# The matmuls of 256 columns take their columns in the order of lines 0, 8, 1, 9 up to 7, 15

## The chip, the cores and the metric

One of the eight cores of a Trainium2 chip runs the whole kernel. The metric is the time of one execution in microseconds (us) of device time, as the median of the runs. TensorE multiplies a stationary tile of weights, loaded beforehand, by a moving tile that streams past, and adds into PSUM; VectorE (DVE), ScalarE (ACT) and GpSimd (POOL) do the elementwise work, and SyncE (SP) issues the loads.

## The reference

Two layers on 256 tokens of width 2048, in float32. All large products have this form, with the weights read once from the chip's main memory:

```python
# layer 1: latent attention beside a gated convolution
h = rmsnorm(x, pre_norm_g)
q_a, c_kv, k_rope, z_mla, c_in, b_gate, c_gate, z_conv, g_mla, g_conv = split(h @ w_in)
q, kv = rmsnorm(q_a) @ w_q_b, rmsnorm(c_kv) @ w_kv_b
attn = causal_attention(q, kv, k_rope) * silu(z_mla)
y_conv = (b_gate * conv3(c_gate * c_in) * silu(z_conv)) @ w_o_conv
merged = sigmoid(g_mla) * (attn @ w_o_mla) + sigmoid(g_conv) * y_conv
x = x + rmsnorm(merged @ w_out, post_norm_g)
# layer 2: 16 meta tokens in front; top-k attention beside a chunked recurrence
h2 = rmsnorm(concat(meta, x))
parts = split(h2 @ w_in_2)
merged = sum over 2 branches of sigmoid(gate) * (y_branch @ w_branch_2)
out = x + merged @ w_out_2
```

## The kernel before

**The numbers.** Every float32 operand of a large product is split into a high and a low part in the format `float32r`, which TensorE takes in one pass, and a product is three matmuls: weights high by x high, weights high by x low, weights low by x high. They add up in one PSUM bank.

**The work in tiles.** The kernel keeps activations transposed: a tile has 128 features on the partitions and the tokens as columns. The tokens are 256 in layer 1 and in most of layer 2 (`S`), and 272 where the meta tokens take part (`T`). `phases` lists the products in order. A phase has groups of up to 512 weight columns, a group has its reduction in tiles of 128 rows, and a unit is what fits 1024 weight columns per partition: mostly two reduction tiles of 512 weight columns. A unit is loaded by SP into one of four slots of `w_raw` (`load`, 512 KB), ACT writes its high part into one of three slots of `w_hi` (`split_hi`, L1616), DVE the low part into `w_lo` (`split_lo`, L1919), and TensorE then runs `tile` (L1290) four times on it, once for each 128 weight columns: 2 reduction tiles of 3 matmuls in each, 24 for the unit. A slot comes free when TensorE is through with its unit.

**Who is stationary.** In the tiles of kind `f` a 128x128 block of weights is stationary and x moves, with 256 or 272 columns. In those of kind `t` (the last product, `wout2`, and half of `kv`) x is stationary and the weights move, with 512 or 256 columns. While a matmul streams, the weights of the next one are loaded beside it. All of them go through the helper `mm`, so the profile has them on L1281.

**Where the operands lie.** A line, here, is 64 bytes of a partition: 16 float32 columns. The allocations are made so:

```python
self.whi = sb("w_hi", [P, N_SPLIT, UNIT], F32R)
self.wlo = sb("w_lo", [P, N_SPLIT, UNIT], F32R)
hb = sb("hb", [P, ODD + 2 * KT * S + ODD], F32R)[:, ODD:ODD + 2 * KT * S]...
self.ob_hi, self.ob_lo = (sb(n, [P, KT, T + ODD], F32R)[:, :, 0:T] for n in ("ob_hi", "ob_lo"))
```

`ODD` is 16 columns, one line. A slot of `w_hi` is 64 lines, a block of weights in it 8 lines. `hb` holds the high and the low part of layer 1's operand, 16 lines a tile, and starts one line into its allocation. A tile of `ob_hi` or `ob_lo` takes 288 columns, 18 lines, of which `operand` (L1136) gives the 256 from column 16 on, or all 272. The results go to a PSUM bank at its start, or, in the phase with eight tiles, to its first or second half (`out_of`, L1149).

**What sets the order.** The whole program is a list of steps that `plan_work` writes once; each engine walks through it and takes the steps of its kind, with semaphores between the engines. Elementwise jobs and the small matmuls of attention and recurrence (plain float32, some of them read in pieces of 1 to 64 columns by `rec_level`) are put between the tiles.

Of the kernel before, what the change touches and what calls it, by code (L numbers as in the profile page):

```python
# [19 lines left out]
S = 256  # L20
# [188 lines left out]
COLS = lambda m: slice(m * P, (m + 1) * P)  # L209
# [831 lines left out]
N_LVL = len(LEVELS) * P // 2  # L1041
L0 = CONSTS["late"][0]

pair = lambda x: x.rearrange("p (h x) -> p h x", h=2)
four = lambda x: x.rearrange("p (a b) -> p a b", a=4)

# [226 lines left out]
def tensor_engine(nc, m, plan, S_):  # L1273
# [6 lines left out]
    def mm(dst, lhsT, rhs, start=True, stop=True):  # L1280
        return nc.tensor.matmul(dst, lhsT, rhs, start=start, stop=stop, skip_group_check=True)  # L1281

    def operand_ready(name, k):
        if name in ("h2", "h2_all"):
            pe.wait_ge(*done["meta"])
            pe.wait_ge(*done["h2", k])
        elif name in ("lat_q", "lat_kv", "oc", "zm", "mg", "ya", "yb", "mg2", "h"):
            pe.wait_ge(*done[name, k])

    def tile(s):  # L1290
        i, t = s.args
        u, slot = plan.units[i], i % N_SPLIT
        hi_w = m.whi[:, slot, 0:u.size].rearrange("p (k n) -> p k n", k=u.nk)
        lo_w = m.wlo[:, slot, 0:u.size].rearrange("p (k n) -> p k n", k=u.nk)
        if t == 0:
            pe.wait_ge(*plan.split[i]["w_lo"])
        if u.k0 == 0:
            pe.wait_ge(*s.of["bank"].after)
        dst = m.out_of(u, t, s.of["bank"].slot)
        kind, j = u.tiles[t][0], int(u.tiles[t][1])  # L1300
        for k in range(u.nk):
            kt = u.k0 + k
            operand_ready(u.phase.operand, kt)
            x_hi, x_lo = m.operand(u.phase.operand, kt)
            first, last = kt == 0 and not (len(u.tiles) > 4 and t % 2), kt == u.phase.ktiles - 1
            if kind == "f":
                inst = mm(dst, hi_w[:, k, COLS(j)], x_hi, first, False)
                inst = mm(dst, hi_w[:, k, COLS(j)], x_lo, False, False)
                inst = mm(dst, lo_w[:, k, COLS(j)], x_hi, False, last)
            else:  # L1310
                w_hi, w_lo, to = hi_w[:, k, :], lo_w[:, k, :], dst
                if u.phase.name == "kv":
                    w_hi, w_lo, to = heads_kv(w_hi), heads_kv(w_lo), pair(dst)
                inst = mm(to, x_hi[:, COLS(j)], w_hi, first, False)
                inst = mm(to, x_lo[:, COLS(j)], w_hi, False, False)
                inst = mm(to, x_hi[:, COLS(j)], w_lo, False, last)
        if u.last:
            inst.then_inc(S_("proj"), 1)
        elif t == len(u.tiles) - 1:
            inst.then_inc(S_("used"), 1)  # L1320
# [261 lines left out]
    def x1_turn(s):  # L1582
# [5 lines left out]
        turn(b[:, P:S], m.xT2[:, k, P:S], ident).then_inc(S_("x1_t"), 1)  # L1588

    does = dict(tile=tile, constants=constants, warm=warm, pre_cols=pre_cols, x_tile=x_tile, row_sum=row_sum, row_spread=row_spread,  # L1590
                cols=cols, angle=angle, meta_turn=meta_turn, rope=rope, scores1=scores1, turn1=turn1, mix1=mix1,
                ki_turn=ki_turn, qa_sum=qa_sum, tok_turn=tok_turn, index=index, scores2=scores2, turn2=turn2,
# [1012 lines left out]
```

## Time and profile before

| | before |
|---|---|
| median of 3 runs | 1965.05 us (1962.56 to 1965.1) |
| the profiled execution's own time | 1960.36 us |
| its span, first to last instruction | 1959.1 us |
| granted TensorE clock over the span | 0.997 of full |
| TensorE matmul busy | 1940.1 us, 99% |
| DVE, ACT, POOL busy | 60%, 45%, 16% |
| loaded from main memory | 335.09 MB, 174 GB/s over the span |

The span is the time between the first and the last instruction on the core; the execution's own time has some 1.3 us more around it. The page gives a matmul's length from its first column to its last result. Matmuls overlap, so a group's mean length is longer than the distance between two starts; that distance is read from the timeline, or from a piece of the chain divided by its count.

### The profile page before, as it was taken

How to read it: one execution, taken by the hardware profiler on the slowest of the kernel's cores; microseconds unless marked ns; L12 is line 12 of the kernel's file. 1: busy time of each engine (PE TensorE's matmuls, PEld its weight loads, DVE VectorE, ACT ScalarE, POOL GpSimd, SP SyncE). 2: the span in 40 equal slices, each digit the busy share in tenths (PEclk: the TensorE clock that was granted, in tenths of full speed). 3: DMA queues.
4: the chain of work that ended last, by engine and by line, in shares of the span. 5: the costliest groups of instructions: out<-in, count | busy, mean ns of one | idle time of the engine just before them, and what ended most of it. 6: DMA issues, size and time to landing. Idle time of an engine off the chain costs nothing.

```text
span 1959.1 us, 37135 instructions
## 1 busy us (share of the span) xinstructions
PE 1940.1 (99%) x15806; PEld 1906.0 (97%) x15806; DVE 1176.2 (60%) x1708; ACT 878.8 (45%) x1264; POOL 319.5 (16%) x320
## 2 busy tenths in 40 slices
PE   8999999999999999999999999999999999999999
PEld 8999999999999999999999999999999999999987
DVE  7765666555554555654564665676467786555644
ACT  6444454544444334444445433455443333444443
POOL 3210010101010002300122253040011232110200
PEclk9999999999999999999999999999999999999999
DMA  7565555556666566666565564444564444566564
GB/s 261 154 194 172 170 151 148 170 178 187 190 183 186 191 184 183 183 194 187 190 227 194 171 205 129 142 140 120 161 179 145 139 141 137 176 195 191 184 229 159
DMA packets 175919, 343.79 MB, mean 175 GB/s; under 512 B 10494, under 2 KB 19578, under 8 KB 175226
## 3 DMA queue, kind: packets, MB, share of 16 engines
q1 hardware_dynamic: 174106, 337.16, 56.5%
q10 hardware_dynamic: 1648, 4.26, 0.6%
q8 instruction: 124, 2.03, 0.4%
q14 instruction: 41, 0.34, 0.1%
HBM read 335.09 MB, written 6.29 MB: 174 GB/s over the span
## 4 chain that ended last, share of the span: by engine, by line
PE 91%; DVE 3%; issue 1%; ACT 1%; POOL 0%; POOLq 0%; DVEq 0%; ACTq 0%
PE bank L1281 91%; DVE w_lo L1919 1%; ACT w_hi L1616 0%; DVE arena L2194 0%; DVE hb L2155 0%; DVE scratch L2025 0%; DVE ob_lo L2199 0%; DVE arena L2188 0%; DVE ob_lo L2130 0%; DVE ob_lo L2155 0%; POOL scratch L2515 0%; PE bank L1498 0%; PE bank L1588 0%; PE bank L1437 0%; PE bank L1438 0%
## 5 line engine op out<-in xcount | busy, mean ns | idle before, releaser
L1919 DVE TENSOR_TENSOR w_lo<-w_raw,w_hi 128x1024 fp32r<-128x1024 f32 (+2 forms) x644 | 786.9, 1226 | 495.3 <-ACT w_hi L1616 493.7
L1616 ACT ACTIVATE w_hi<-w_raw 128x1024 fp32r<-128x1024 f32 (+2 forms) x644 | 662.5, 1032 | 894.7 <-PE bank L1281 888.7
L1281 PE MATMUL bank<-hb,w_hi 128*128 128x256 f32 x4896 | 870.1, 281 | 3.4 <-DVE w_lo L1919 3.3
L1281 PEld LDWEIGHTS bank<-hb,w_hi 128*128 128x128 f32 x4896 | 748.7, 188 | 6.3 <-DVE w_lo L1919 5.0
L1281 PE MATMUL bank<-hb,w_lo 128*128 128x256 f32 x2448 | 684.2, 280 | 0.0
L1281 PE MATMUL bank<-ob_hi,w_hi 128*128 128x256 f32 (+1 forms) x2224 | 643.0, 289 | 4.4 <-DVE w_lo L1919 3.9
L1281 PE MATMUL bank<-ob_lo,w_hi 128*128 128x256 f32 (+1 forms) x2224 | 627.0, 282 | 0.0
L1281 PE MATMUL bank<-ob_hi,w_lo 128*128 128x256 f32 (+1 forms) x2224 | 626.2, 282 | 0.0
L1281 PEld LDWEIGHTS bank<-hb,w_lo 128*128 128x128 f32 x2448 | 460.8, 188 | 0.0
L1281 PEld LDWEIGHTS bank<-ob_hi,w_hi 128*128 128x128 f32 x2224 | 419.6, 189 | 8.1 <-DVE w_lo L1919 5.4
L1281 PEld LDWEIGHTS bank<-ob_lo,w_hi 128*128 128x128 f32 x2224 | 419.5, 189 | 1.5
L1281 PEld LDWEIGHTS bank<-ob_hi,w_lo 128*128 128x128 f32 x2224 | 419.0, 188 | 0.0
L1281 PE MATMUL bank<-arena 128*128 128x64 f32 (+4 forms) x618 | 101.7, 302 | 2.6 <-ACT arena L1836 1.6
L1281 PEld LDWEIGHTS bank<-arena 128*128 128x128 f32 x618 | 81.0, 191 | 4.8 <-ACT arena L1836 2.3
L2525 POOL TENSOR_TENSOR arena<-scratch,arena 128x256 f32<-128x256 f32 x32 | 38.4, 1229 | 269.7 <-DVE scratch L2025 269.7
L2025 DVE TENSOR_TENSOR scratch<-bank,factor 128x256 f32<-128x256 f32 (+1 forms) x132 | 52.8, 422 | 38.1 <-PE bank L1281 38.0
L1281 PE MATMUL bank<-w_hi,ob_hi 128*128 128x512 f32 (+1 forms) x192 | 69.0, 360 | 0.0
L1281 PE MATMUL bank<-w_lo,ob_hi 128*128 128x512 f32 (+1 forms) x192 | 68.5, 357 | 0.0
L1281 PE MATMUL bank<-w_hi,ob_lo 128*128 128x512 f32 (+1 forms) x192 | 68.2, 355 | 0.0
L2498 POOL TENSOR_TENSOR arena<-arena,factor 128x256 f32<-128x256 f32 x16 | 19.2, 1233 | 268.9 <-DVE arena L2025 268.9
L2515 POOL TENSOR_TENSOR scratch<-scratch,head_factor 128x256 f32<-128x256 f32 x16 | 12.6, 786 | 238.7 <-ACT head_factor L1729 238.7
L2025 DVE TENSOR_TENSOR arena<-bank,factor 128x256 f32<-128x256 f32 (+1 forms) x86 | 34.5, 420 | 23.6 <-PE bank L1281 23.6
(240 smaller groups left out, 1174.0 us busy)
## 6 DMA issues: line engine op xcount, KB each, us to landing
w_raw<-in_w_in SPq DMA_DIRECT2D x436, 512.0 KB, 3.7
w_raw<-in_w_out SPq DMA_DIRECT2D x64, 512.0 KB, 4.2
w_raw<-in_w_o_conv SPq DMA_DIRECT2D x32, 512.0 KB, 3.9
w_raw<-in_w_o_mla SPq DMA_DIRECT2D x32, 512.0 KB, 4.1
w_raw<-in_w_branch SPq DMA_DIRECT2D x32, 512.0 KB, 3.8
w_raw<-in_w_kv_b SPq DMA_DIRECT2D x16, 512.0 KB, 3.7
w_raw<-in_w_q_b SPq DMA_DIRECT2D x16, 384.0 KB, 3.3
arena<-x_kept SPq DMA_DIRECT2D x2, 2048.0 KB, 10.1
```

The source lines that it names most:

```text
L1281: return nc.tensor.matmul(dst, lhsT, rhs, start=start, stop=stop, skip_group_check=True)
L1616: act(dst, src, ACT.Copy).then_inc(S_("w_hi"), 1)
L1919: tt(low, src, high.bitcast(F32), ALU.subtract).then_inc(S_("w_lo"), 1)
L2025: tt(dst, m.proj[s.of["pb"]][:, 0:dst.shape[1]], factor, ALU.mult).then_inc(S_("evac"), 1)
L2498: tt(m.u_t[:, t, :], m.u_t[:, t, :], m.R, ALU.mult).then_inc(S_("conv_b"), 1)
L2515: tt(z, z, ring[s.of["head"].slot][:, 0:S], ALU.mult).then_inc(S_("silu"), 1)
L2525: tt(y, m.scratch[s.of["scratch"].slot][:, 0:S], y, ALU.add).then_inc(S_("merged"), 1)
```

## The change

The columns of a moving tile of 256 are viewed as two halves of eight lines, and the access pattern goes over line, half, column within the line: line 0, line 8, line 1, line 9, up to line 7, line 15. The PSUM tile is viewed in the same way, so each result lands at the address it had before. It holds for all tiles of kind `f` with 256 columns. Those with 272 columns keep their order (in `twos`, a tile whose second dimension isn't `S` is handed back as it is), and so do those of kind `t`. The program has the same instructions in the same order on every engine.

```diff
+twos = lambda x: x.rearrange("p (b a e) -> p a b e", b=2, e=16) if x.shape[1] == S else x
 pair = lambda x: x.rearrange("p (h x) -> p h x", h=2)
...
             if kind == "f":
-                inst = mm(dst, hi_w[:, k, COLS(j)], x_hi, first, False)
-                inst = mm(dst, hi_w[:, k, COLS(j)], x_lo, False, False)
-                inst = mm(dst, lo_w[:, k, COLS(j)], x_hi, False, last)
+                x_hi, x_lo, to = twos(x_hi), twos(x_lo), twos(dst)
+                inst = mm(to, hi_w[:, k, COLS(j)], x_hi, first, False)
+                inst = mm(to, hi_w[:, k, COLS(j)], x_lo, False, False)
+                inst = mm(to, lo_w[:, k, COLS(j)], x_hi, False, last)
```

## Rows read from the trace of the kernel before

**Rows 1.** The page: engines and their busy share, granted clock by slice, chain by engine.

```profile
PE 1940.1 (99%) x15806; PEld 1906.0 (97%) x15806; DVE 1176.2 (60%) x1708; ACT 878.8 (45%) x1264; POOL 319.5 (16%) x320
...
PEclk9999999999999999999999999999999999999999
...
PE 91%; DVE 3%; issue 1%; ACT 1%; POOL 0%; POOLq 0%; DVEq 0%; ACTq 0%
```

**Rows 2.** The chain in order of time: start us, length us, what; its four longest pieces.

```profile
79.53 108.86 PE bank L1281 x918
...
388.05 163.46 PE bank L1281 x1384
...
561.44 239.63 PE bank L1281 x2040
...
832.54 257.56 PE bank L1281 x2212
```

**Rows 3.** Waits of TensorE: us in total, times, longest us; the costliest.

```profile
PE bank L1281 <- DVE w_lo L1919: 7.1, 7, 2.8
```

**Rows 4.** Groups by shape: matmuls; count | busy us, mean ns of one | idle us before.

```profile
L1281 PE MATMUL bank<-hb,w_hi 128*128 128x256 f32 x4896 | 870.1, 281 | 3.4 <-DVE w_lo L1919 3.3
...
L1281 PE MATMUL bank<-hb,w_lo 128*128 128x256 f32 x2448 | 684.2, 280 | 0.0
...
L1281 PE MATMUL bank<-ob_hi,w_hi 128*128 128x256 f32 x1824 | 521.2, 286 | 4.4 <-DVE w_lo L1919 3.9 <-DVE ob_lo L2199 0.4
L1281 PE MATMUL bank<-ob_lo,w_hi 128*128 128x256 f32 x1824 | 511.8, 281 | 0.0
L1281 PE MATMUL bank<-ob_hi,w_lo 128*128 128x256 f32 x1824 | 510.6, 280 | 0.0
...
L1281 PE MATMUL bank<-ob_hi,w_hi 128*128 128x272 f32 x400 | 121.8, 305 | 0.0
```

**Rows 5.** Timeline, TensorE, near 1323 and 1472 us: start us, us for all xcount.

```profile
1323.35 0.49 PE L1498 MATMUL bank<-con,prob 128*128 128x128 f32 x3
...
1472.24 1.00 PE L1281 MATMUL bank<-arena 128*128 128x64 f32 x8
```

**Rows 6.** Groups by shape again: the f32 matmuls of 64 and 128 columns.

```profile
L1281 PE MATMUL bank<-arena 128*128 128x64 f32 x224 | 28.1, 268 | 1.1 <-POOL arena L2555 1.1
L1281 PE MATMUL bank<-arena 128*128 128x128 f32 x192 | 26.0, 275 | 0.0
...
L1498 PE MATMUL bank<-con,prob 128*128 128x128 f32 x24 | 3.9, 273 | 0.0
```

**Rows 7.** Timeline, TensorE, 1141 us, first and last of five starts.

```profile
1141.12 0.42 PE L1281 MATMUL bank<-ob_lo,w_hi 128*128 128x256 f32 x1
...
1141.97 0.42 PE L1281 MATMUL bank<-ob_hi,w_lo 128*128 128x256 f32 x1
```

**Rows 8.** Busy time in windows: us, busy of each engine (x), PEclk, DMA share, GB/s.

```profile
1141.50:1142.50 1.00, 1.00 (x7) 1.00 (x6) 0.32 (x1) 0.00 (x0) 0.90 (x1) 0.56 0.52 131
1144.50:1145.50 1.00, 1.00 (x11) 1.00 (x10) 1.00 (x1) 0.11 (x1) 0.00 (x0) 1.00 1.26 312
```

**Rows 9.** Timeline, TensorE, 1106 us, first and last of 18 starts.

```profile
1105.96 0.28 PE L1281 MATMUL bank<-ob_hi,w_hi 128*128 128x256 f32 x1
...
1107.89 0.28 PE L1281 MATMUL bank<-ob_hi,w_lo 128*128 128x256 f32 x1
```

**Rows 10.** Groups by shape: the two halves of a weight unit on DVE and ACT.

```profile
L1919 DVE TENSOR_TENSOR w_lo<-w_raw,w_hi 128x1024 fp32r<-128x1024 f32 x612 | 767.0, 1256 | 494.3 <-ACT w_hi L1616 492.7
...
L1616 ACT ACTIVATE w_hi<-w_raw 128x1024 fp32r<-128x1024 f32 x612 | 647.5, 1059 | 873.2 <-PE bank L1281 867.2 <-DMA w_raw<-in_w_out 5.5
```

**Rows 11.** Timeline, TensorE, last phase, first and last of 14 starts.

```profile
1919.95 0.39 PE L1281 MATMUL bank<-w_hi,ob_lo 128*128 128x512 f32 x1
...
1922.98 0.40 PE L1281 MATMUL bank<-w_lo,ob_hi 128*128 128x512 f32 x1
```

## The prediction

> **What bounds the kernel now.** I read the share of busy time first: TensorE is busy for 99% of the span and its granted clock stands at 2.4 GHz in nearly every slice [rows 1]. Busy time alone proves little, since matmuls overlap, so the chain of work that ended last comes next. It runs over TensorE for 91% of the span, through the one line that issues the matmuls [rows 1]. Of the waits of TensorE that the trace names, the largest sum is 7.1 us in 7 waits, for the low halves of the weights [rows 3]. So the time is the number of matmuls times the distance between two starts, and only that distance can change much.
>
> The matmuls that the change touches are those with a moving tile of 256 columns. The groups by shape give 4896 + 2448 on `hb` and 3 x 1824 on `ob_hi` and `ob_lo`, together **12,816** [rows 4]. The 280 ns that such a row shows is the length of one from first column to last result; what counts is the distance of starts. Four long pieces of the chain hold almost nothing else: 108.86 + 163.46 + 239.63 + 257.56 = 769.51 us for 918 + 1384 + 2040 + 2212 = 6554 matmuls, or **117.4 ns** each [rows 2].
>
> What could it be? Two rows give a floor. Three transposes in a row, each of which loads 128 columns of weights and streams 128 columns of f32, take 0.49 us; with the last one's own length of 273 ns taken off, 2 distances make 0.217 us, **109 ns** each [rows 5, 6]. Eight matmuls that stream only 64 columns behind a weight load of 128 take 1.00 us, or 105 ns each with the last one's 268 ns off, so it is the weight load that counts there [rows 5, 6]. Each matmul of 256 columns also has one weight load of 128 columns beside it, so 109 ns is what the weight side allows. The moving side: in the short stretch where the granted clock fell to 1.2 GHz (0.56 on the mean of that microsecond) [rows 8], four distances of the same 256-column shape make 0.85 us, 212.5 ns, which is 256 columns at 1.2 GHz and nothing more [rows 7]. At 2.4 GHz this is 106.3 ns. So at the slow clock there is no excess over the columns, and at the fast clock there is one of 8 ns over the floor of 109. Something that has slack at half pace has none at full pace.
>
> And the excess isn't fixed. In the stretch from 1105.96 to 1107.89 us, 17 distances of this shape, with the same kind of tiles and the same program line, make 1.93 us: 113.5 ns [rows 9]. The piece x1384 of the chain stands at 118.1 ns [rows 2]. Two steady rhythms for one instruction say that the cost is a collision between two streams whose relative position can differ, and not a price of the instruction.
>
> **The change, part by part.** No instruction is added, removed or moved, on any engine or queue; no wait changes. Each of the 12,816 matmuls streams the same 256 columns, as 16 lines of 16 columns (64 bytes) in another order, and puts its results down in the same order, so that each lands where it did. The kinds with 272 columns (1200) and with `ob` as the stationary side (576) stay as they are. Three things are to be costed:
>
> *Order of the reads.* While one matmul streams 16 lines, the weights of the next are loaded from 8 lines. In the order of before the moving stream crosses two lines in the time of one weight line, so the two sweep over each other. In the new order it is in lines j and j + 8 while the weight load is in line j: the distance between them stays the same modulo 8. The code's sizes fix that distance. A weight tile begins at a multiple of 8 lines from the start of `w_hi`, and `hb` begins one line further on (`ODD`); a row of `ob` is 288 columns, 18 lines, and is read from column 16. So relative to the weights the moving tile begins at an odd line in all cases. If the store serves lines by turns of two, four or eight, and collisions of the two readers are what costs the 8 ns, then the streams never meet in step. No row shows that the store is divided in this way; it is my reading of [rows 7, 9]. Its value is bounded from both sides. If the excess goes wholly, 12,816 x (117.4 - 109) = 108 us; if they meet all the time instead of half of it, the excess would double, and 108 us would be lost. The value I take lies at the floor of [rows 5], since those matmuls show a weight load and a stream beside it that cost nothing together: 108 us.
>
> *Order of the writes, and the pieces themselves.* 15 breaks in the address of a matmul, on both sides. The nearest row on reads: the matmuls of 64 columns from `arena`, 224 of them, are read in pieces of 1, 2, 4 up to 64 columns and last 268 ns on the mean, against 275 for 128 columns in one piece [rows 6], and follow each other at 105 ns [rows 5]. If f32 streams a column in 0.83 ns, as [rows 5] suggest (109 ns for 128), 64 columns take 53, so up to 52 ns for 63 breaks, 0.8 ns per break, could be hidden there. The price of a break is thus between 0 and 0.8 ns on the read side, and on the write side no row shows one at all, so the same two ends have to serve, and below nothing for a write order that collides less. I take 0: it is what the rows show where they show anything. Both ends go into the rivals.
>
> The Trainium skill speaks against this (PSUM — Partial Sum Buffer, section Specifications (TRN2)): "any non-contiguous AP slows matmuls significantly". The page gives no price; by that rule the sum would be a loss, and what it would do here is the last rival below. No run here writes PSUM in pieces, so the trace neither bears it out nor refutes it.
>
> *What a faster TensorE asks of the others.* 24 matmuls of a weight unit take 2.82 us now and would take 2.62. In that time DVE needs 1.26 us for the low half and ACT 1.06 for the high half, plus evictions [rows 10]; a 512 KB load in 2.62 us is 200 GB/s, and the queue moved 312 GB/s in the microsecond when it caught up [rows 8]. So the feeders hold, except where they're already late: the stretches of the recurrence and of the index, where TensorE waits for DVE and POOL. The chain spends 9% of the span off TensorE [rows 1], in such places; I take as large a share of the gain as swallowed there, 10 us of the 108. The sum is **-98 us**.
>
> The profiled execution took 1960.4 us; 98 less is 1862. The median of the three runs is 4.7 us above it, so the forecast for the median is **1867 us**.
>
> **The rivals.**
>
> *Only the better rhythm.* The new order makes the streams settle in the rhythm of [rows 9], because part of the excess is something else, a line change in the moving stream say. For it: this rhythm is seen to be stable. Against: nothing says why a new order should stop there. 12,816 x (117.4 - 113.5) = 50 us less: 1915.
>
> *The order is of no matter.* The excess may belong to the moving stream or to the accumulation alone. For it: matmuls of 512 columns also have one weight load each, 8 lines, yet 13 distances from 1919.95 to 1922.98 us make 3.03 us, 233 ns against 213 for the columns at 2.4 GHz [rows 11]; an excess over the columns of 20 ns, twice the 11 of a matmul of 256. If the weight load were the only thing to collide with, the second half of such a matmul would be free of it. Against: the two rhythms. Time: 1965.
>
> *Slower, by the pieces.* TensorE's results are written in 16 pieces, and a break costs the writer, or the address generator, up to the 0.8 ns that is left open above: 15 x 0.8 = 12 ns per matmul. It decides from 8.4 / 15 = 0.56 ns per break on if the whole excess goes, and from any price if none goes. With the gain, 109 + 12 = 121, so 12,816 x 3.6 = 46 us more: 2011; without it 12,816 x 12 = 154 us more: 2119. For it speaks that a break on the write side is nowhere seen to be free; against it, that a piece of 16 columns is long and in [rows 5, 6] pieces of one column cost nothing visible.
>
> **How the numbers follow.** A run of this kernel can be told from another from about 0.2%, 4 us, on. Whole excess gone: 0.55 (1850 to 1888; the lower end is the full 108 us with nothing given back, and some microseconds under it for a floor nearer to the 106.3 ns of the columns). Better rhythm: 0.14 (about 1888 to 1950). No matter: 0.11 (1950 to 1969). Slower: 0.20 (nearly all of it for the pieces, the rest for streams that always meet). The first three hold 8 in 10 together, so the range is 1850 to 1970. Faster takes the first two, 0.69; same most of the third, 0.10; slower the rest, 0.21.
>
> **What would show each step.** In the trace of the changed kernel the long pieces of the chain should read about 109 to 110 ns per matmul where they read 117.4, and both rhythms should be gone; the 272-column and 512-column rows should be what they are. The waits of TensorE for the low halves should grow by some microseconds (10 in all the engine's waits). Pieces that read 113.5 speak for the second case, 117 for the third, anything over 118 for a price of the breaks; a longer time with pieces at 109 would mean that I misjudged the feeders.

## The result, and the profile after

The changed kernel is slower: 2001.64 us as the median of 4 runs (2001.42 to 2003.24), against 1963.8 us for the kernel before beside it (1957.14 to 1965.1, 4 runs). The ratio is 1.0206, with a 95% interval of 1.0184 to 1.0228. The forecast was 1867 us. The profiled execution took 2001.82 us, its span is 2000.5 us, 41.4 us more than the span of before.

The page of the changed kernel, engines and chain, the view of [rows 1]:

```profile
PE 1984.1 (99%) x15806; PEld 1951.5 (98%) x15806; DVE 1174.9 (59%) x1708; ACT 879.3 (44%) x1264; POOL 318.9 (16%) x320
...
PE 95%; DVE 2%; ACT 1%; issue 1%; DMA 1%; POOL 0%; SPq 0%; POOLq 0%; ACTq 0%
```

TensorE gained 44 us of busy time in its matmuls and 45.5 in its weight loads, the other engines none; its share of the chain rose from 91 to 95%. Its long pieces in the chain, in order of time (start us, length us, what), the view of [rows 2]:

```profile
82.41 112.12 PE bank L1282 x918
...
397.87 721.49 PE bank L1282 x5984
...
1673.93 244.87 PE bank L1282 x1969
```

They read 122.1, 120.6 and 124.4 ns per matmul, where before had 117.4 on the mean of four. The first can be set beside [rows 2] directly: the same 918 matmuls, 228 of them not touched by the change, stood at 118.6. The last holds 60 matmuls of 512 columns, so its 124.4 isn't the distance of one shape. The groups by shape (count | busy us, mean ns of one | idle us before), the view of [rows 4]:

```profile
L1282 PE MATMUL bank<-hb,w_hi 128*128 128x256 f32 x4896 | 892.3, 285 | 2.9 <-DVE w_lo L1921 2.9
...
L1282 PE MATMUL bank<-hb,w_lo 128*128 128x256 f32 x2448 | 693.9, 283 | 0.0
L1282 PE MATMUL bank<-ob_hi,w_hi 128*128 128x256 f32 x1824 | 530.9, 291 | 2.6 <-DVE w_lo L1921 2.6
L1282 PE MATMUL bank<-ob_lo,w_hi 128*128 128x256 f32 x1824 | 520.4, 285 | 0.0
...
L1282 PE MATMUL bank<-ob_hi,w_hi 128*128 128x272 f32 x400 | 121.6, 304 | 0.0
```

Each shape of 256 columns is 3 to 5 ns longer than in [rows 4]; the one of 272, which the change leaves alone, isn't. The waits for the low halves were fewer than in [rows 3]:

```profile
PE bank L1282 <- DVE w_lo L1921: 5.5, 4, 2.9
```

A slower TensorE leaves more time for the low halves, but that this is why isn't shown: the kernel with the writes alone in pieces, as fast as the one before, also has fewer waits (6.3 us in 5).

The clearest view is the timeline of TensorE on `hb` around 600 us, the first and the last of nine rows that begin a group of three matmuls:

```profile
599.74 0.40 PE L1282 MATMUL bank<-hb,w_hi 128*128 128x256 f32 x2
...
602.62 0.40 PE L1282 MATMUL bank<-hb,w_hi 128*128 128x256 f32 x2
```

24 distances make 2.88 us: 120.0 ns, and so it goes on. When all distances between starts in the two timelines are sorted by operand, with those over 145 ns (a wait, or a small matmul between) set aside:

| moving operand | distances | before, mean ns | after, mean ns |
|---|---|---|---|
| `hb`, 256 columns | 7260 | 116.98 | 120.02 |
| `ob_hi`, 256 columns | 3550 | 117.13 | 120.81 |
| `ob_lo`, 256 columns | 1820 | 116.90 | 122.51 |
| `ob_hi`, 272 columns | 753 | 126.20 | 126.14 |
| weights, 512 columns | 375 | 232.26 | 232.23 |

On `hb`, 7173 of the 7259 distances after are exactly 120 ns, where before had 117, 118 and 119 for the most part and 113 and 114 for 1285 of 7260. The three changed rows give 22 + 13 + 10 = 45 us more. The distances set aside give 4 us back: 196 of them, 54.9 us in sum, became 174 and 48.2 us, and the 22 that left are now ordinary ones. So the 41 us of the span are accounted for, all by the distance between starts.

### The profile page after: what moved, and what is told of

It reads as the page before. It is cut to its first block, busy times and chain, and to the rows that moved or that the text cites. A ratio compares the mean times of both kernels' runs of the same rounds, so it can differ in the third digit from the quotient of the medians.

```text
span 2000.5 us, 37135 instructions
## 1 busy us (share of the span) xinstructions
PE 1984.1 (99%) x15806; PEld 1951.5 (98%) x15806; DVE 1174.9 (59%) x1708; ACT 879.3 (44%) x1264; POOL 318.9 (16%) x320
## 4 chain that ended last, share of the span: by engine, by line
PE 95%; DVE 2%; ACT 1%; issue 1%; DMA 1%; POOL 0%; SPq 0%; POOLq 0%; ACTq 0%
PE bank L1282 94%; DVE w_lo L1921 1%; ACT w_hi L1618 1%; DMA w_raw<-in_w_in 1%; DVE arena L2196 0%; DVE ob_lo L2201 0%; DVE arena L2190 0%; POOL scratch L2517 0%; PE bank L1500 0%; DVE arena L1940 0%; ACT scratch L1632 0%; PE bank L1590 0%; PE bank L1438 0%; PE bank L1439 0%; PE bank L1440 0%
## 5 line engine op out<-in xcount | busy, mean ns | idle before, releaser
L1282 PE MATMUL bank<-hb,w_hi 128*128 128x256 f32 x4896 | 892.3, 285 | 2.9 <-DVE w_lo L1921 2.9
L1282 PEld LDWEIGHTS bank<-hb,w_hi 128*128 128x128 f32 x4896 | 763.6, 191 | 4.8 <-DVE w_lo L1921 3.4
L1282 PE MATMUL bank<-hb,w_lo 128*128 128x256 f32 x2448 | 693.9, 283 | 0.0
L1282 PE MATMUL bank<-ob_hi,w_hi 128*128 128x256 f32 (+1 forms) x2224 | 652.6, 293 | 2.6 <-DVE w_lo L1921 2.6
L1282 PE MATMUL bank<-ob_lo,w_hi 128*128 128x256 f32 (+1 forms) x2224 | 635.4, 286 | 0.0
L1282 PEld LDWEIGHTS bank<-hb,w_lo 128*128 128x128 f32 x2448 | 468.2, 191 | 0.0
L1282 PEld LDWEIGHTS bank<-ob_hi,w_lo 128*128 128x128 f32 x2224 | 423.6, 190 | 0.0
```

## The experiments

Two kinds were run: the full kernel with one thing changed, and small kernels that leave the computation out and run stretches of 72 matmuls with nothing else on the core, so that the distance can be read by itself. In the small kernels a block of weights begins a multiple of 8 lines from the start of `w_hi`, and the allocation of the moving tiles a multiple of 64 lines from it; the offset is the number of lines at which the moving tile begins in its allocation. A distance is the length of a stretch over 72. Each small kernel was executed once, at a granted clock of 0.994 to 0.996 of full. The ratios of the full kernels are to the kernel before run beside them, with a median of 1961.98 or 1962.18 us.

**Small kernel 1.** Its core:

```python
xh, xl = x[:, at:at + n], x[:, 4096 + at:4096 + at + n]     # at = 16 * (offset + 16 * tile)
mm(hi, xh, k == 0, False)
mm(hi, xl, False, False)
mm(lo, xh, False, k == 1)                                    # rd(x) and wr(dst) are plain or in pieces
```

> This kernel leaves out the whole computation; it runs stretches of 72 matmuls each (float32r, weight blocks and 256-column moving tiles laid out as in the kernel), and in each stretch one thing differs: the piece length and order of the reads, of the writes, of both, the line at which the moving tile begins relative to the weights (0 to 7), the number of weight columns, the number of moving columns. Theory A, pieces: every piece costs one beat of 1.2 GHz (0.83 ns) at its end whatever its place, because in the changed kernel 7173 of the 7259 undisturbed distances on hb are exactly 120 ns = (128 + 16) x 0.83. It expects 120 at all eight offsets with 16 pieces, 133 with 32 pieces (8 columns each), 113.3 with 8 pieces, 110 with 4, and the same for any order of the pieces, also with fewer weight columns. Theory B, meeting: the new order makes the moving stream meet the weight stream all the time. It expects the distance to change with the offset (up to 117 or more at some, 109 at others) and to fall when 64 or 32 weight columns are loaded instead of 128. Theory C, the writes alone: reads in pieces stay at 117 or less, writes in pieces alone give 120. For the plain order all theories expect 113 to 118; if the excess over 109 there comes from the weight load, it goes when 32 weight columns are loaded.

From the timeline of TensorE in small kernel 1 (start us, us for the count), the row that begins a stretch, and the one that begins the next, so that two rows enclose 72 distances. Rows 1 to 5: plain order, offsets 0, 1, 2, 3, and the begin of 4. Rows 6 and 7: reads and writes in 16 pieces, offset 1. Rows 8 to 10: reads alone, then writes alone. Rows 11 and 12: plain order with 32 weight columns instead of 128 (`128*32`). Rows 13 and 14: reads and writes in pieces with 32 weight columns. Rows 14 and 15: the writes alone in pieces with 64 weight columns.

```profile
42.66 0.40 PE L137 MATMUL bank<-hb,w_hi 128*128 128x256 f32 x2
...
51.30 0.40 PE L137 MATMUL bank<-hb,w_hi 128*128 128x256 f32 x2
...
59.78 0.40 PE L137 MATMUL bank<-hb,w_hi 128*128 128x256 f32 x2
...
68.33 0.40 PE L137 MATMUL bank<-hb,w_hi 128*128 128x256 f32 x2
...
76.51 0.39 PE L137 MATMUL bank<-hb,w_hi 128*128 128x256 f32 x2
...
118.98 0.41 PE L137 MATMUL bank<-hb,w_hi 128*128 128x256 f32 x2
...
127.62 0.40 PE L137 MATMUL bank<-hb,w_hi 128*128 128x256 f32 x2
...
179.47 0.41 PE L137 MATMUL bank<-hb,w_hi 128*128 128x256 f32 x2
...
188.11 0.40 PE L137 MATMUL bank<-hb,w_hi 128*128 128x256 f32 x2
...
196.59 0.40 PE L137 MATMUL bank<-hb,w_hi 128*128 128x256 f32 x2
...
374.73 0.39 PE L137 MATMUL bank<-hb,w_hi 128*32 128x256 f32 x2
...
382.89 0.40 PE L137 MATMUL bank<-hb,w_hi 128*96 128x256 f32 x2
...
400.23 0.40 PE L137 MATMUL bank<-hb,w_hi 128*32 128x256 f32 x2
...
408.87 0.40 PE L137 MATMUL bank<-hb,w_hi 128*64 128x256 f32 x2
...
417.28 0.40 PE L137 MATMUL bank<-hb,w_hi 128*64 128x256 f32 x2
```

The four offsets take 8.64, 8.48, 8.55 and 8.18 us; the pieces 8.64, whether read and written or read alone, the writes alone 8.48; with 32 weight columns it's 8.16 plain and 8.64 in pieces; the writes alone with 64 weight columns take 8.41. As steady means, each without its first 24 distances:

| stretch | offset 0 | 1 | 2 | 3 |
|---|---|---|---|---|
| plain order, ns | 120.0 | 117.8 | 118.7 | 113.3 |
| read and written in 16 pieces, ns | 120.0 | 120.0 | 120.0 | 120.0 |
| reads alone in pieces, ns | 120.0 | 120.0 | | |
| writes alone in pieces, ns | 120.0 | 117.8 | | |

Offsets 4 to 7 read as 0 to 3. At offset 1 with 96, 64 or 32 weight columns the plain order takes 113.3 ns each time; the pieces still take 120.9, 120.0 and 120.0.

So three things are apart now. Reads in these 16 pieces take 120.0 ns wherever they begin, and no less when fewer weights are loaded beside them. The plain order takes 113.3 ns with fewer weight columns, and up to 120.0 with all 128, by the offset modulo four lines. That the weight load is in its way is the nearest reading, but fewer weight columns also mean fewer partitions of results, and this kernel doesn't tell the two apart. And writes in pieces cost nothing with 128 weight columns, at the two offsets tried. With 64 weight columns they do: 116.7 ns, where the plain order has 113.3. So they can cost the plain order its good distance.

Four numbers of the expectation missed, all by the theory of one beat per piece. Pieces of 8 columns took 123.3 ns and not 133; 8 and 4 pieces took 118.7 and 117.8 at offset 1 and not 113.3 and 110; and the order 0, 4, 8, 12, 1, 5 and on took 118.9, so the order of the pieces does matter.

**The two sides in the full kernel.** Reads alone in pieces, from the changed kernel:

```diff
-                x_hi, x_lo, to = twos(x_hi), twos(x_lo), twos(dst)
+                x_hi, x_lo, to = twos(x_hi), twos(x_lo), dst
```

> The reads are in pieces, the results are written in plain order (so the columns of the products change places, which only the values notice). Theory A, the price is on the read side, one beat of 0.83 ns per piece, as the stretches of the small kernel showed (120.0 ns with reads in pieces, 117.8 with writes in pieces): 2001 us, like the changed kernel, with 120 ns on hb. Theory C, the writes cost: 1964. Both sides share it: about 1982.

Writes alone:

```diff
-                x_hi, x_lo, to = twos(x_hi), twos(x_lo), twos(dst)
+                to = twos(dst)
```

> The reads are in plain order, the results are written in pieces (the columns of the products change places). Theory A, the reads cost and the writes are free: 1964 us, like the kernel before, distances of 113 and 118 ns on hb in about the same shares. Theory C, the writes cost: 2001.

Reads alone: 2001.62 us, ratio 1.0195 (1.018 to 1.0211). Writes alone: 1960.23 us, ratio 0.9993 (0.9981 to 1.0005). The chain of waits of the first:

```profile
80.77 112.12 PE bank L1282 x918
...
396.23 721.50 PE bank L1282 x5984
```

and of the second:

```profile
79.88 108.85 PE bank L1282 x918
...
561.99 239.62 PE bank L1282 x2040
```

The pieces of the chain are those of the changed kernel (112.12, 721.49) and of the kernel before (108.86, 239.63 in [rows 2]) to a hundredth. On `hb` the writes alone have 117.40 ns against 116.98, 3 us in sum; that is less than the runs of one kernel differ here. The whole price in the full kernel is on the read side.

**The offset in the full kernel.** Plain order, `hb` three lines beyond the weights instead of one, by another order of the allocations (small tensors of an odd number of lines stand before it):

```diff
-        hb = sb("hb", [P, ODD + 2 * KT * S + ODD], F32R)[:, ODD:ODD + 2 * KT * S].rearrange("p (k n) -> p k n", k=2 * KT)
+        self.stats = [sb(f"stats{i}", [P, 8])[:, :] for i in range(6)]
+        hb = sb("hb", [P, 2 * KT * S], F32R)[:, :].rearrange("p (k n) -> p k n", k=2 * KT)
+        small3, self.q_factor = sb("small3", [P, 2 * HI]), sb("q_factor", [P, 2 * HA])
...
-        self.stats = [sb(f"stats{i}", [P, 8])[:, :] for i in range(6)]
...
-        self.small2, small3 = sb("small2", [P, 64]), sb("small3", [P, 2 * HI])
-        self.q_factor = sb("q_factor", [P, 2 * HA])
+        self.small2 = sb("small2", [P, 64])
```

> The kernel before, plain order, but hb begins three lines past the weights modulo 4 instead of one, by another order of the allocations; nothing else moves. Theory D, the excess of the plain order is a meeting of the moving stream with the weight load that depends on the offset modulo four lines (the small kernel: 120.0, 117.8, 118.7, 113.3 ns at offsets 0, 1, 2, 3, the same at 4 to 7): the 7260 undisturbed distances on hb go from 117.0 to 113.3 ns, 27 us less, 1937 us. Rival: in the full kernel the rhythm is set by what disturbs it (waits, other engines' accesses), and both rhythms stay mixed: 1955 to 1965.

1938.17 us, ratio 0.9878 (0.9862 to 0.9895). The mean distance on `hb` fell from 116.98 to 113.66 ns, on `ob_hi` and `ob_lo` it stayed at 117.08 and 116.75. From its timeline, around 590 us on `hb`, first and last of 13 rows that begin a group of three matmuls:

```profile
589.79 0.39 PE L1281 MATMUL bank<-hb,w_hi 128*128 128x256 f32 x2
...
593.87 0.39 PE L1281 MATMUL bank<-hb,w_hi 128*128 128x256 f32 x2
```

36 distances make 4.08 us, 113.3 ns. The changed kernel with the same allocations:

> The changed kernel with the same shift of hb to three lines. Theory A, a read in 16 pieces takes 144 beats wherever it begins (120.0 ns at all eight offsets in the small kernel): hb stays at 120 ns and the time at 2001 us. Theory B, the changed kernel is slow because the two streams always meet at the offset of one line: hb falls below 117 ns and the time to 1975 or less.

2002.41 us, ratio 1.0201 (1.0186 to 1.0216); `hb` stays at 120.02 ns. The offset is worth 24 us to the plain order and nothing to the pieces.

**Small kernel 2: how a piece costs.**

> Leaves out the whole computation, like the first small kernel; stretches of 72 matmuls. Theory A, a piece is dear because its end breaks the address: 16 pieces of one line each that lie in rising order with gaps between them (pitch of 17, 20, 32 or 48 columns) also take 120 ns, at offsets 1 and 3 alike; two pieces (pitch 144 for 128 columns) cost nothing to speak of. Theory E, the order of lines is what costs and not the break: pieces with a pitch of 17 or 20 columns take what the plain order takes, 113 to 118. With 32 weight columns loaded: 113.3 for the plain order at every offset; pieces of 8, 16, 32, 64 columns then give their own price without the weight load: 126.7 or less, 120, 116.7, 115 if it is one beat per piece over the 17 x 8 beats of the plain order's 113.3 less the 8 that it has already; if the plain order's 8 extra beats are one per two lines, pieces of 32 and 64 columns stay at 113.3. The weights shifted by 1, 2, 3, 4 lines under an hb at offset 1: the relative offset counts, so 120, 113.3, 118.7, 117.8. Fractions of a line between offsets 2 and 4: no distance under 113.3 is expected, since 17 x 6.67 ns looks like the least for 16 lines. Tiles 18 lines apart beginning at offset 3: 117 to 118, as the offset is 3 and 1 by turns; 20 lines apart: 113.3.

From its timeline, the first row of each stretch. Two rows for pieces that lie in rising order, 16 columns each at a pitch of 20, offset 1; two rows for two pieces of 128 columns at a pitch of 144, offset 3; then, all with 32 weight columns, the two-stream order in pieces of 8, 16, 32 and 64 columns, the orders 0, 4, 8, 12, 1, 5 and on, and 0, 2, 4 up to 14, 1, 3 and on, and the end; last, in plain order at offset 3 with 128 weight columns, moving tiles of 192 and of 128 columns, and the end:

```profile
53.37 0.40 PE L137 MATMUL bank<-hb,w_hi 128*128 128x256 f32 x2
...
62.01 0.41 PE L137 MATMUL bank<-hb,w_hi 128*128 128x256 f32 x2
...
131.17 0.40 PE L137 MATMUL bank<-hb,w_hi 128*128 128x256 f32 x2
...
139.79 0.40 PE L137 MATMUL bank<-hb,w_hi 128*128 128x256 f32 x2
...
148.33 0.41 PE L137 MATMUL bank<-hb,w_hi 128*32 128x256 f32 x2
...
157.21 0.40 PE L137 MATMUL bank<-hb,w_hi 128*32 128x256 f32 x2
...
165.84 0.40 PE L137 MATMUL bank<-hb,w_hi 128*32 128x256 f32 x2
...
174.25 0.39 PE L137 MATMUL bank<-hb,w_hi 128*32 128x256 f32 x2
...
182.43 0.40 PE L137 MATMUL bank<-hb,w_hi 128*32 128x256 f32 x2
...
190.83 0.40 PE L137 MATMUL bank<-hb,w_hi 128*32 128x256 f32 x2
...
199.47 0.40 PE L137 MATMUL bank<-hb,w_hi 128*128 128x256 f32 x2
...
503.58 0.37 PE L137 MATMUL bank<-hb,w_hi 128*128 128x192 f32 x2
...
511.61 0.35 PE L137 MATMUL bank<-hb,w_hi 128*128 128x128 f32 x2
...
519.62 0.45 PE L137 MATMUL bank<-hb,w_hi 128*128 128x256 f32 x2
```

The gap of four columns between pieces in rising order brings 8.64 us, 120.0 ns: it takes no strange order for the price, an end that the next column doesn't follow is enough. The stretches with 32 weight columns take 8.88, 8.63, 8.41, 8.18, 8.40 and 8.64 us; their steady means are 123.3, 120.0, 116.7, 113.3 (the plain order's), 116.7 and 120.0 ns. Against 113.3 the 16 pieces cost 0.42 ns each and 8 pieces of 32 columns as much, but 32 pieces of 8 only 0.31, 4 pieces of 64 nothing, and 16 pieces that jump by four lines half as much as those that jump by eight or by two. So the number of pieces is the main thing, and the distance of the jump has a say that no rule here covers.

Several expectations missed. The gaps: 16 pieces at a pitch of 17, 20, 32 and 48 columns took 124.5, 120.0, 122.2 and 120.0 ns at offset 1 and 124.4, 120.0, 120.0 and 117.8 at offset 3, where 120 was due for all. Two pieces of 128 columns with a gap of one line took 117.4 ns at offset 1, but 120.0 at offset 3 (8.62 us above), where the plain order has 113.3. So a piece has no fixed price while 128 weight columns are loaded; the 0.42 ns holds for the stretches with 32. The offset: with the weights shifted under the tile, relative offsets 0, 3, 2, 1 gave 120.0, 117.8, 118.7, 117.8 ns, and a tile at offset 3 over weights shifted by four lines 117.8, where 113.3 was due for 3 (the blocks of weights come in another order there too). Tiles 20 lines apart at offset 3 gave 117.8 as well. In the first four of the shifted stretches the moving tiles stayed where they were and the distance changed with the weights alone, so their place takes part. Offset 3 allows the good rhythm and doesn't compel it; in the other direction, the first stretch of small kernel 1, at offset 1, ran at 113.3. Inside a line the offset matters too: 2.25 lines gave 113.3 and 3.25 gave 119.2, and even with 32 weight columns a tile that began at 0.5 or 1.5 lines took 117.4 and 117.5, so the weight load is not the whole of the plain order's excess. And 512 columns at offset 0 took 226.7 ns with 128 weight columns and 231.7 with 32: what slows the matmuls of 512 columns isn't the weight load alone. Last, the moving tiles of 192 and 128 columns took 8.03 and 8.01 us, both 111.7 ns in the steady part: with so few columns it's the 128 weight columns that set the distance.

**Small kernel 3: what has slack.**

> Leaves out the whole computation. Part one: 16 stretches of plain 256-column matmuls at offsets 0, 1, 2, 3 by turns, each after a stretch of 512 columns that upsets the rhythm. If the offset alone decides, all four stretches of an offset read alike: 120.0, 117.8, 118.7, 113.3; if two rhythms are stable at the odd offsets and chance decides, stretches of 1 and 3 read 113.3 or 117.8. Part two: pieces at half pace, in f32 (256 columns, plain, and in pieces of 16, 8, 32, 1 columns). Theory A, a break costs beats of the read that half pace hides: 213 to 216 ns in all, at least down to 8 columns. If a break stops the stream itself: 16 pieces add 6.7 ns or more here too. Part three: two-byte operands (bf16) at full pace, plain and in pieces of 64, 32, 16, 8 columns, which halve the bytes. If the 113.3 of the plain order is a limit of bytes or lines read, plain falls to 109 to 111; if it is a limit of columns, it stays at 113. If the price goes with the number of pieces, 16 pieces still add about 6.7 ns; if it goes with lines touched, pieces of 16 columns (half a line each) add less.

The offsets came out alike in all four rounds: 120.0, 117.8, 118.5, 113.3. Its timeline inside a stretch merges equal matmuls (start us, us for all with the last one's own length, count): f32 plain, f32 in pieces of 16 columns, f32 in pieces of one column, then bf16 plain and bf16 in pieces of 16:

```profile
409.72 15.49 PE L137 MATMUL bank<-w_raw 128*128 128x256 f32 x71
...
440.80 15.49 PE L137 MATMUL bank<-w_raw 128*128 128x256 f32 x71
...
533.69 15.74 PE L137 MATMUL bank<-w_raw 128*128 128x256 f32 x57
...
567.25 5.95 PE L137 MATMUL bank<-xb 128*128 128x256 bf16 x53
...
590.83 6.39 PE L137 MATMUL bank<-xb 128*128 128x256 bf16 x57
```

Plain f32 streams 256 columns in 215.8 ns a pass, and 16 pieces cost it nothing; only at one column a piece does it reach 273. With two-byte operands a matmul takes 109.2 ns, plain and in every kind of pieces down to 8 columns. Among the forms tried, the price, and the excess of the plain order too, shows only where TensorE takes four bytes per column at full pace. For the excess of the plain order the bf16 stretches leave a second reading: their weight loads are shorter too, 98 ns against 188 in the trace.

**Fewer pieces.** The changed kernel with `e=32`, and with `e=64`:

> The changed kernel with pieces of 32 columns (two lines): 8 pieces instead of 16. Theory A with the price by the number of pieces: the small kernel had 118.8 ns at offset 1 for this shape; from 117.0 that is 1.8 ns on 12,600 matmuls, 23 us: 1985 us. If any break sends the read to 144 beats: 2001.

> The changed kernel with pieces of 64 columns (four lines): 4 pieces. The small kernel had 117.8 ns at offset 1, which is the plain order's slower rhythm: between 1962 (both rhythms as before) and 1972 us (all of it at 117.8).

1979.41 us, ratio 1.0089 (1.0065 to 1.0114), and 1963.73 us, ratio 1.0006 (0.9993 to 1.0019). On `hb` 118.70 and 117.40 ns. 16, 8 and 4 pieces stand in the full kernel as in the small ones; the 32-column form came out 6 us below what I had expected, mostly since `ob` rose only to 118.1 to 118.4 ns and not by the full 1.8.

**A version faster than both.** The allocations of `hb_third_line`, and those operands in `ob` that share no row with the 272-column one laid 16 lines apart, all at offset 3. They feed 2016 of the 5472 matmuls on `ob`, and half of them had offset 3 before. Its main lines:

```diff
+        ob = [sb(n, [P, KT * (T + ODD)], F32R) for n in ("ob_hi", "ob_lo")]
+        self.ob_hi, self.ob_lo = (o[:, :].rearrange("p (k n) -> p k n", k=KT)[:, :, 0:T] for o in ob)
+        self.eb_hi, self.eb_lo = (o[:, NMETA:NMETA + KT * S].rearrange("p (k n) -> p k n", k=KT) for o in ob)
...
-        return self.ob_hi[:, k, NMETA:T], self.ob_lo[:, k, NMETA:T]
+        return self.eb_hi[:, k, :], self.eb_lo[:, k, :]
```

> As hb_third_line, and the operands of 256 columns that share the ob allocation with the 272-column one (lat_q, lat_kv, oc, zm) lie 16 lines apart, all at the offset of three lines, instead of 18 lines apart with offsets of 3 and 1 by turns: 2016 more matmuls at the good offset. Theory D: their distance goes from 117.1 to about 113.7 ns, 7 us less than hb_third_line: 1931 us. Rival: the two rhythms are a matter of chance on ob and nothing moves: 1938.

1932.89 us, ratio 0.9863 (0.9838 to 0.9887). The distance on `ob_hi` and `ob_lo` fell to 116.04 and 115.79 ns, that of the 512-column matmuls, whose stationary operand moved too, to 229.11. Against `hb_third_line` the interval leaves it open whether the last step is a gain; against the kernel before, both are.

## Why the prediction was wrong

The forecast was 1867 us in a range of 1850 to 1970; the median is 2001.64. Two terms of the sum failed: the gain of 8.4 ns per matmul from the order of the reads didn't come, and the price of the breaks, put at 0, turned the sign. Point by point, by its own steps.

*What bounds the kernel* held. The distance between starts on TensorE sets the time, and 41 us of distances make 41 us of span.

*The floor of 109 ns* is the first step that failed: "The value I take lies at the floor of [rows 5], since those matmuls show a weight load and a stream beside it that cost nothing together". Those rows stream f32, at half pace (215.8 ns for 256 columns in small kernel 3). At full pace a plain read of 256 columns of `float32r` takes 113.3 ns even with 32 weight columns beside it, and 109.2 only with two-byte operands. The weight side was read too low as well. The 105 ns for the eight matmuls of 64 columns is the mean of one short distance and six long ones, as a narrower window of the same timeline shows:

```profile
1472.24 0.33 PE L1281 MATMUL bank<-arena 128*128 128x64 f32 x2
```

With the last one's own 0.27 us off, the first distance is 0.06 us; the other six share 0.67 us, some 112 ns each, and 128 weight columns took 111.7 in small kernel 2. So at most 117.4 - 113.3 = 4.1 ns a matmul were there to gain, 53 us, and not the 8.4 ns and 108 us of the sum. The rival with the better rhythm had the size of that right.

*The two rhythms* as a meeting with the weight load: the runs bear this out in the main. At offset 1 the excess goes with 96 or fewer weight columns, and with 128 it depends on the offset. But a tile that begins at half a line keeps 4 ns of it with 32 weight columns, so it isn't the whole. What follows from it is to choose the offset, not the order. The pieces took 120.0 ns with the weight load and nearly without it, so there is no telling whether their streams meet.

*The price of a break* is the step that turned the sign: "I take 0: it is what the rows show where they show anything." Again the rows were f32 at half pace, where 16 pieces are free (215.8 ns). At full pace they cost 6.7 ns over the 113.3, 0.42 ns per piece or 0.44 per break, which lies inside the ends that I kept (0 and 0.8) and under the 0.56 from which I had it decide; that threshold was wrong because it counted on 8.4 ns of gain; with 4.1 it is 0.27. The right sum is 120.02 - 116.98 = 3.0 ns on `hb`, 3.7 and 5.6 on `ob`, 41 us in all with the waits. Why `ob` pays more than 120.0 isn't traced to the end; tiles 18 lines apart gave 121.7 in small kernel 1 too.

*The rival that came true* is the slower one, with 2011 us; measured are 2002. Its distance, 121 ns, is near to 120 to 122.5, but two errors made that up: a floor too low by 4 ns and a price too high by 5. And it looked at the writers first: "TensorE's results are written in 16 pieces". The Trainium skill (PSUM — Partial Sum Buffer, section Specifications (TRN2)) has it there too, that any non-contiguous access slows matmuls significantly. The full kernel with the writes alone in pieces, 0.9993, says no for pieces of 64 bytes, and the small kernel for 32 bytes as well with 128 weight columns; with 64 weight columns the writes in pieces took 116.7 ns against 113.3. On the read side the Trainium skill (SBUF — State Buffer, section Door 1: The DMA port swizzle) names lines of 16 bytes and asks for two hits or more on each for full bandwidth; pieces of 64 bytes obey that and cost 6.7 ns here. For both the measurement decides.

*The feeders* weren't put to the test by a slower TensorE, and only in part by a faster one. In `hb_third_line` the distances on `hb` fell by 24 us in sum and the span by 23, so about 1 us was given back, and not the tenth that the prediction took. The 3 us missing to the 27 of that run's expectation are mostly the distance itself, 113.66 ns and not 113.3. The waits for the low halves stood at 8.8 us in 11 waits against 7.1 in 7. What a gain of 108 us would have met stays open.

## What to carry to other kernels

A bound on a cost holds only for the pace at which its rows ran: the same access was free at half pace and 6% of a matmul at full pace, so look for rows that run the resource as hard as the change will. Where matmuls stream four-byte operands at full pace, read them in long runs. Four runs of 256 bytes cost nothing in the full kernel, eight of 128 bytes 0.9%, sixteen of 64 bytes 2%; but a long run is no warrant, since two of 512 bytes with a gap of one line took 120.0 ns where one run took 113.3. The order of the writes cost nothing in the full kernel. If their distance has two values, try where the moving tile begins relative to the weights: moving an allocation by two lines of 64 bytes gave 1.2% here, and reordering the reads took 2%.

## What the runs showed of the hardware

- Matmuls of 256 `float32r` columns follow each other at 113.3, 117.8, 118.7 or 120.0 ns by the offset between moving tile and weights in whole lines of 64 bytes, with a period of four lines; between whole lines other values occur (119.2 at 3.25). 113.3 and 120.0 are 17 and 18 times 6.67 ns, the time of one such line at full pace, for a tile of 16 lines. Why one or two lines' time is added isn't shown.
- The same instruction with the same offset can hold either of two rhythms for a hundred matmuls and more (offset 1, 128 weight columns, tiles 16 lines apart: 113.3 in the first stretch of small kernel 1, 117.8 in the others).
- With 128 weight columns and 128 to 224 moving ones, all `float32r`, the distance is 111.7 ns whatever the number of moving columns, so the weight load sets it.
- Two-byte operands take 109.2 ns in any of the tried orders. The Trainium skill (TensorE: Matmul & The Clock Gate, section Back-to-back issue gap) gives N / 2.4 + 2.5 ns for matmuls by themselves, 109.2 for 256 columns; that agrees for bf16, even with weight loads of 128 columns beside them, and falls 4 ns short for `float32r`.
- Open: whether the end of a piece costs, or the jump, or both (a jump of four lines cost half of one of two or eight), and why 512 columns of `float32r`, 213.3 ns of streaming at 2.4 GHz, take 226.7 to 233.3 ns with an offset of 0 to 3, and don't get faster with fewer weight columns.
